# Normed input's two tiles put 96 bytes behind the weights' addresses modulo 128, not 64

## The chip, the cores and the metric

The kernel runs on one core of a Trainium2 chip. The metric is the device time of one execution in microseconds; smaller is better. [...]

## What is computed

Two transformer blocks in float32 on 256 tokens of width 1024, one after the other. The first mixes four branches (a state-space scan and three attentions), the second runs two layers, HGRN2 and then a gated linear recurrence (RG-LRU). Each mixer is followed by a SwiGLU feed-forward of width 2816. Nearly all of the arithmetic is products of a normed input with a large weight matrix:

```python
def rmsnorm(x, w):
    xf = x.astype(jnp.float32)
    y = xf * lax.rsqrt(jnp.mean(xf * xf, axis=-1, keepdims=True) + NORM_EPS)
    return (y * w.astype(jnp.float32)).astype(x.dtype)
...
def swiglu(h, w_gate, w_up, w_down):
    return (jax.nn.silu(h @ w_gate) * (h @ w_up)) @ w_down
...
    h = rmsnorm(x, norm_mix[l])
    x = x + hybrid_mixer(h, w_in[l], ...)
    h = rmsnorm(x, norm_ffn[l])
    x = x + swiglu(h, w_ffn_gate[l], w_ffn_up[l], w_ffn_down[l])
```

## The kernel before

**Weights in units.** Every weight matrix is cut into units (`unit`, `cols`, L210 to L290) of at most 2048 floats in each of 128 partitions, 1 MB. SyncE loads them in order, in two halves, into three rotating slots of the tile `raw` (L2142 to L2160). ScalarE rounds a half to the type fp32r in `whi` (L958), VectorE, or GpSimd in the feed-forwards, puts the rest `raw - whi` in `wlo` (L1359, L1947). The input is split in the same way into a high part and a low part: `hh` and `hl` for the normed input of every mixer and feed-forward (written at L990 and L1383), `bh` and `bl` for the branches' outputs, `eh` and `el` for the inputs of two output products, `ch` and `cl` for a third, `gh` and `gl` for the down products. A product of float32 accuracy is the sum of three fp32r products: high by high, high by low, low by high.

**Two forms of a product.** A matmul loads one operand of 128 x 128 into the array and streams the other past it. In `still` (L480 to L501) the weights are loaded and the input is streamed, 256 columns (the tokens) at a time; its three passes are L492, L495 and L500. A unit of 256 weight columns takes 48 matmuls. `project_columns` and `project_pair` use it on `hh`, `hl` for 112 units and for the half-width unit `dk` (24 matmuls), and `branch` uses it on `bh`, `bl` for 8 units. In `moving` (L503 to L521) the input is loaded and the weights are streamed, 512 columns at a time; its passes are L512, L516 and L520. `project_tokens` uses it on `hh`, `hl` (`z`, `cv`, `bv`, and two each of `hv` and `hg`; two units each, 24 matmuls a unit), and `add_product` on `eh`, `ch` and `gh`. The weights for the next matmul are loaded while the current one streams.

**Order.** Each engine runs its own program; semaphores join them. TensorE goes through the units in order. A feed-forward first has 22 units in the form `still` (the first two as `project_pair`, the other 20 in one stream with the end of that pair: 984 matmuls without other work between), then 11 units in the form `moving`. In the first mixer the streams are short, since attention scores, transposes and value products stand between the units.

**Addresses.** `sbuf` takes tiles from one stack in the order of the calls, each right behind the one before (L84 to L164). All weight slots begin at multiples of 128 bytes in a partition, and all slices that matmuls take of these tiles are multiples of 512 bytes apart, so a tile's address modulo 128 holds for all of its operands. Modulo 128 the tiles begin at: `raw`, `whi`, `wlo`, `x`, `hn`, `eh`, `el` 0; `hh`, `hl` 64 (behind `gap_hh`, 64 bytes); `wrow`, `ident`, `vec`, `st` 64; `diag` and `half` 32; `gate`, `gh`, `gl` 0 (behind `gap_stage`, 288 bytes); `bh`, `bl` 64 (behind `gap_bh`); `ch`, `cl` 0 and `uc` 96; `gw` 0.

Of the kernel before, what the change touches and what calls it, by code (L numbers as in the profile page):

```python
# [72 lines left out]
def build(nc, a):  # L73
    V, A, G, T, S = nc.vector, nc.scalar, nc.gpsimd, nc.tensor, nc.sync
    vq, aq, gq, tq, sq = Waits(V), Waits(A), Waits(G), Waits(T), Waits(S)
    with ExitStack() as root:
# [3 lines left out]
        def sbuf(ctx, name, shape, dt=f32):  # L80
            return ctx.enter_context(nc.sbuf_tensor(name, shape, dt))
# [8 lines left out]
        eh = sbuf(shifted, "eh", [128, 8, 256], f32r)  # L90
        el = sbuf(shifted, "el", [128, 8, 256], f32r)
        shifted.close()
        sbuf(root, "gap_hh", [128, 16])
        hh = sbuf(root, "hh", [128, 8, 256], f32r)
        hl = sbuf(root, "hl", [128, 8, 256], f32r)
        wrow = sbuf(root, "wrow", [128, 2, D])
# [2 lines left out]
        st = sbuf(root, "st", [128, 24])  # L99
        diag = sbuf(root, "diag", [128, 2, 128])  # L100
        half = sbuf(root, "half", [128, 16])
        sbuf(root, "gap_stage", [128, 72])
        banks = [root.enter_context(nc.psum_tensor(f"bank{i}", [128, 512], f32)) for i in range(8)]

        mix = ExitStack()
# [2106 lines left out]
```

## Time and profile before

| | |
|---|---|
| time, median of 3 runs | 1138.95 us (1138.86 to 1139.53) |
| time of the profiled execution | 1138.59 us |
| its span, first to last instruction | 1137.4 us |
| TensorE busy | 1122.9 us, 8117 matmuls |
| VectorE, ScalarE, GpSimd busy | 660.1, 574.5, 297.1 us |
| HBM read | 205.01 MB, 184 GB/s over the span |

Matmuls overlap each other in the array: one is listed from its first to its last part, some 280 ns for 256 columns, though the next begins much sooner. How fast the stream goes is read from the starts in the timeline.

### The profile page before, as it was taken

The page shows a single profiled execution, that of the slowest core. Times are in us where ns is not written, and L with a number is a line of the kernel's source. Part 1 is how long each engine was busy: PE and PEld are TensorE (multiplying, and loading weights), DVE is VectorE, ACT ScalarE, POOL GpSimd, SP SyncE. Part 2 cuts the span into 40 slices and gives each one's busy share as a digit, 9 for nine tenths or more (in the row PEclk, how much of TensorE's full clock was granted, in tenths as well). Part 3 has the DMA queues.
Part 4 walks back from the last instruction along what each step waited for, and adds up shares of the span by engine and source line. Part 5 has one row for each costly group of instructions (what it writes and reads, how often), then busy time and mean ns, then how long its engine had stood idle before and what let it go on. Part 6 is the DMA issues. An engine that isn't in the chain of part 4 may idle for free.

```text
span 1137.4 us, 19300 instructions
## 1 busy us (share of the span) xinstructions
PE 1122.9 (99%) x8117; PEld 1044.9 (92%) x8117; DVE 660.1 (58%) x1039; ACT 574.5 (51%) x878; POOL 297.1 (26%) x193
## 2 busy tenths in 40 slices
PE   8999999999999999999999999999999999999997
PEld 7899989999989999889998889999889979999986
DVE  6755765677675454338897665343238797434324
ACT  6646555555454644436732445444335855544432
POOL 3022100000005444422421114444510003444440
PEclk9999999999999999999999999999999999999999
DMA  8679474554647666655543358665556255765550
GB/s 273 205 250 326 141 241 138 175 153 134 209 151 211 180 188 201 203 185 153 186 165 112 111 164 268 210 189 189 191 180 188 91 182 152 218 189 187 187 183 37
DMA packets 155152, 207.48 MB, mean 182 GB/s; under 512 B 9471, under 2 KB 128409, under 8 KB 155066
## 3 DMA queue, kind: packets, MB, share of 16 engines
q1 hardware_dynamic: 151274, 193.11, 54.2%
q0 software_dynamic: 3792, 13.15, 3.5%
q8 instruction: 64, 1.05, 0.4%
q14 instruction: 22, 0.18, 0.1%
HBM read 205.01 MB, written 4.24 MB: 184 GB/s over the span
## 4 chain that ended last, share of the span: by engine, by line
PE 89%; DVE 7%; ACT 3%; issue 1%; DMA 0%; POOL 0%; SPq 0%; DVEq 0%; ACTq 0%
PE bank L492 18%; PE bank L495 18%; PE bank L500 18%; PE bank L520 9%; PE bank L516 9%; PE bank L512 9%; PE bank L861 3%; DVE wlo L1359 2%; PE bank L787 1%; PE bank L797 1%; ACT whi L958 1%; DVE area L1507 1%; PE bank L562 1%; PE bank L809 1%; DVE uc L1507 0%
## 5 line engine op out<-in xcount | busy, mean ns | idle before, releaser
L1359 DVE TENSOR_TENSOR wlo<-raw,whi 128x1024 fp32r<-128x1024 f32 x275 | 336.2, 1250 | 232.4 <-ACT whi L958 231.6
L958 ACT ACTIVATE whi<-raw 128x1024 fp32r<-128x1024 f32 x362 | 360.5, 1044 | 113.8 <-PE bank L520 107.1
L1947 POOL TENSOR_TENSOR wlo<-raw,whi 128x1024 fp32r<-128x1024 f32 x87 | 223.2, 2565 | 253.8 <-ACT whi L958 253.8
L492 PE MATMUL bank<-hh,whi 128*128 128x256 f32 x1784 | 285.1, 281 | 0.0
L495 PE MATMUL bank<-hh,wlo 128*128 128x256 f32 x1784 | 281.7, 279 | 0.0
L500 PE MATMUL bank<-hl,whi 128*128 128x256 f32 x1784 | 281.5, 279 | 0.0
L492 PEld LDWEIGHTS bank<-hh,whi 128*128 128x128 f32 x1784 | 241.4, 188 | 3.3 <-issue 2.7
L495 PEld LDWEIGHTS bank<-hh,wlo 128*128 128x128 f32 x1784 | 240.8, 188 | 0.0
L500 PEld LDWEIGHTS bank<-hl,whi 128*128 128x128 f32 x1784 | 240.6, 188 | 0.0
L1954 POOL TENSOR_TENSOR st<-st,half 128x1 f32<-128x1 f32 x18 | 10.8, 609 | 334.0 <-DVE st L1376 301.8
L512 PE MATMUL bank<-whi,gh 128*128 128x512 f32 x264 | 81.4, 390 | 0.0
L516 PE MATMUL bank<-wlo,gh 128*128 128x512 f32 x264 | 81.4, 389 | 0.0
L520 PE MATMUL bank<-whi,gl 128*128 128x512 f32 x264 | 81.3, 389 | 0.0
L1188 ACT ACTIVATE sg<-sg 128x512 f32<-128x512 f32 x33 | 20.8, 632 | 95.6 <-DVE sg L1406 95.6
L1192 ACT ACTIVATE gh<-sg 128x512 fp32r<-128x512 f32 x33 | 20.8, 630 | 86.0 <-DVE sg L1740 86.0
L520 PEld LDWEIGHTS bank<-whi,gl 128*128 128x128 f32 x264 | 49.6, 188 | 10.4
L516 PEld LDWEIGHTS bank<-wlo,gh 128*128 128x128 f32 x264 | 49.6, 188 | 10.3
L512 PEld LDWEIGHTS bank<-whi,gh 128*128 128x128 f32 x264 | 49.2, 188 | 9.9
L1740 DVE TENSOR_TENSOR sg<-sg,bank 128x512 f32<-128x512 f32 x33 | 22.7, 688 | 57.4 <-PE bank L500 55.4
L1406 DVE TENSOR_TENSOR sg<-bank,bc_f 128x512 f32<-128x512 f32 x33 | 22.7, 689 | 46.7 <-PE bank L500 46.7
L983 ACT ACTIVATE bank<-x_sb 128x512 f32<-128x512 f32 x26 | 15.6, 600 | 57.6 <-DVE x_sb L1428 29.9
L1742 DVE TENSOR_TENSOR gl<-sg,gh 128x512 fp32r<-128x512 f32 x33 | 30.8, 932 | 23.3 <-ACT gh L1192 23.3
(313 smaller groups left out, 1225.7 us busy)
## 6 DMA issues: line engine op xcount, KB each, us to landing
raw<-in_ffn_w_in SPq DMA_DIRECT2D x88, 512.0 KB, 3.8
raw<-in_w_in SPq DMA_DIRECT2D x72, 512.0 KB, 4.8
raw<-in_ffn_w_out SPq DMA_DIRECT2D x44, 512.0 KB, 3.3
raw<-in_hgrn_w_in SPq DMA_DIRECT2D x32, 512.0 KB, 4.2
raw<-in_w_ffn_gate SPq DMA_DIRECT2D x22, 512.0 KB, 4.7
raw<-in_w_ffn_up SPq DMA_DIRECT2D x22, 512.0 KB, 4.3
raw<-in_w_ffn_down SPq DMA_DIRECT2D x22, 512.0 KB, 3.3
raw<-in_w_branch SPq DMA_DIRECT2D x16, 512.0 KB, 4.4
```

The costliest lines, as they stand in the source:

```text
L492: T.matmul(out, wh[:, i, c], xh[:, k, :], start=first and (i, k) == pairs[0], stop=False)
L495: T.matmul(out, wl[:, i, c], xh[:, k, :], start=False, stop=False)
L500: t = T.matmul(out, wh[:, i, c], xl[:, k, :], start=False, stop=last and (i, k) == pairs[-1])
L512: tok = T.matmul(out, xh[:, k, r], wh[:, i, c], start=first and i == 0, stop=False)
L516: tok = T.matmul(out, xh[:, k, r], wl[:, i, c], start=False, stop=False)
L520: tok = T.matmul(out, xl[:, k, r], wh[:, i, c], start=False, stop=last and i == len(ks) - 1)
L861: tok = T.matmul(banks[b][:, 128 * (2 * h + t):128 * (2 * h + t) + 128], kj[:, h, c], qj[:, h, c], start=True, stop=True)
L958: A.activation(half_of(whi, j, h), half_of(raw, j, h), ACT.Copy).then_inc(s_hi[j % NS][h], 1)
L1359: V.tensor_tensor(half_of(wlo, j, h), half_of(raw, j, h), half_of(whi, j, h).bitcast(f32), ALU.subtract).then_inc(s_lo[j % NS][h], 1)
L1406: V.tensor_tensor(dst, two(bank_of("col", *key)[:, :]), bc[:, :].rearrange("p (o t) -> p o t", o=1).broadcast_to([128, 2, 256]), ALU.mult) ...
L1742: V.tensor_tensor(gl[:, 2 * j:2 * j + 2, :], two(s), gh[:, 2 * j:2 * j + 2, :].bitcast(f32), ALU.subtract).then_inc(s_gl, 1)
L1947: G.tensor_tensor(half_of(wlo, j, 1), half_of(raw, j, 1), half_of(whi, j, 1).bitcast(f32), ALU.subtract).then_inc(s_lo[j % NS][1], 1)
```

## The change

The unused tile `gap_hh` in front of `hh` has 24 floats in place of 16, and `gap_stage` 64 in place of 72. `hh`, `hl`, `wrow`, `ident`, `vec`, `st`, `diag` and `half` begin 32 bytes later; `gate` and all that follows stay where they were. Instructions, waits and transfers are the same.

```diff
@@ -90,7 +90,7 @@
         eh = sbuf(shifted, "eh", [128, 8, 256], f32r)
         el = sbuf(shifted, "el", [128, 8, 256], f32r)
         shifted.close()
-        sbuf(root, "gap_hh", [128, 16])
+        sbuf(root, "gap_hh", [128, 24])
         hh = sbuf(root, "hh", [128, 8, 256], f32r)
         hl = sbuf(root, "hl", [128, 8, 256], f32r)
         wrow = sbuf(root, "wrow", [128, 2, D])
@@ -99,7 +99,7 @@
         st = sbuf(root, "st", [128, 24])
         diag = sbuf(root, "diag", [128, 2, 128])
         half = sbuf(root, "half", [128, 16])
-        sbuf(root, "gap_stage", [128, 72])
+        sbuf(root, "gap_stage", [128, 64])
```

## Rows read from the trace of the kernel before

**Rows 1.** The page: head, TensorE's busy us and share, granted clock by slice.

```profile
span 1137.4 us, 19300 instructions
...
PE 1122.9 (99%) x8117; PEld 1044.9 (92%) x8117; DVE 660.1 (58%) x1039; ACT 574.5 (51%) x878; POOL 297.1 (26%) x193
...
PEclk9999999999999999999999999999999999999999
```

**Rows 2.** The page: the chain that ended last, by engine and by line.

```profile
PE 89%; DVE 7%; ACT 3%; issue 1%; DMA 0%; POOL 0%; SPq 0%; DVEq 0%; ACTq 0%
PE bank L492 18%; PE bank L495 18%; PE bank L500 18%; PE bank L520 9%; PE bank L516 9%; PE bank L512 9%; PE bank L861 3%; DVE wlo L1359 2%; PE bank L787 1%; PE bank L797 1%; ACT whi L958 1%; DVE area L1507 1%; PE bank L562 1%; PE bank L809 1%; DVE uc L1507 0%
```

**Rows 3.** Waits of PE, longest first: us in total, times, longest us.

```profile
PE bank L632 <- DMA wrow<-in_norm_mix: 2.2, 1, 2.2
PE bank L640 <- DVE hn L1470: 1.8, 1, 1.8
```

**Rows 4.** Timeline (start us, length us, matmuls merged): `still`, first feed-forward.

```profile
344.71 0.63 PE L492 MATMUL bank<-hh,whi 128*128 128x256 f32 x4
...
458.72 0.63 PE L500 MATMUL bank<-hl,whi 128*128 128x256 f32 x4
```

**Rows 5.** Timeline: `still` on the same tiles, in the first mixer.

```profile
174.31 0.62 PE L495 MATMUL bank<-hh,wlo 128*128 128x256 f32 x4
...
177.48 0.62 PE L500 MATMUL bank<-hl,whi 128*128 128x256 f32 x4
```

**Rows 6.** Timeline: `still` on `bh` and `bl`, two streams.

```profile
188.11 0.40 PE L492 MATMUL bank<-bh,whi 128*128 128x256 f32 x2
...
189.52 0.40 PE L492 MATMUL bank<-bh,whi 128*128 128x256 f32 x2
...
195.40 0.39 PE L492 MATMUL bank<-bh,whi 128*128 128x256 f32 x2
...
196.76 0.28 PE L492 MATMUL bank<-bh,whi 128*128 128x256 f32 x1
```

**Rows 7.** Timeline: `moving` with `hh` loaded, product `z`.

```profile
41.95 1.09 PE L516 MATMUL bank<-wlo,hh 128*128 128x512 f32 x4
...
45.68 1.09 PE L520 MATMUL bank<-whi,hl 128*128 128x512 f32 x4
```

**Rows 8.** Timeline: `moving` with `gh` loaded, first down product.

```profile
461.94 0.62 PE L512 MATMUL bank<-whi,gh 128*128 128x512 f32 x2
...
464.66 0.62 PE L512 MATMUL bank<-whi,gh 128*128 128x512 f32 x2
```

**Rows 9.** Timeline: `moving` with `eh` loaded, behind a group of transposes.

```profile
657.42 0.63 PE L516 MATMUL bank<-wlo,eh 128*128 128x512 f32 x2
...
660.20 0.62 PE L516 MATMUL bank<-wlo,eh 128*128 128x512 f32 x2
...
661.12 0.61 PE L512 MATMUL bank<-whi,eh 128*128 128x512 f32 x2
...
662.48 0.61 PE L512 MATMUL bank<-whi,eh 128*128 128x512 f32 x2
```

**Rows 10.** By line: duration ns (min/median/max), first and last start us.

```profile
L492 PEld LDWEIGHTS bank<-hh,whi x1784: 186/188/192, 17.5 to 1070.1; 128*128 128x128 f32 x199
L492 PE MATMUL bank<-hh,whi x1784: 276/279/467, 17.6 to 1070.2; 128*128 128x256 f32 x199
...
L512 PEld LDWEIGHTS bank<-whi,gh x264: 187/188/192, 459.1 to 1129.8; 128*128 128x128 f32 x132
L512 PE MATMUL bank<-whi,gh x264: 389/389/476, 459.2 to 1130.0; 128*128 128x512 f32 x132
...
L512 PE MATMUL bank<-whi,hh x128: 228/394/483, 35.6 to 641.8; 128*128 128x512 f32 x112, 128*128 128x144 f32 x16
...
L929 PE MATMUL bank<-uc,gw x64: 377/379/379, 883.3 to 896.9; 128*128 128x256 f32 x64
```

**Rows 11.** Stretches: length us, each engine's busy us, clock, DMA share, GB/s.

```profile
343.40:459.10 115.70, 115.70 (x985) 115.70 (x984) 57.05 (x78) 60.25 (x71) 54.99 (x22) 1.00 0.65 193
460.50:514.90 54.40, 54.40 (x242) 45.04 (x241) 19.07 (x19) 20.96 (x27) 18.33 (x7) 1.00 0.57 184
```

## The prediction

> **What bounds the kernel now.** The page's head and busy lines come first [rows 1]: a span of 1137.4 us, in which TensorE streams matmuls for 1122.9 us (99%). [...] The chain that ended last says the same thing by line: 89% of it is PE, and L492, L495 and L500, the three passes of `still`, hold 18% each [rows 2]. The waits of TensorE are small: the longest two are 2.2 and 1.8 us [rows 3]. So the time is the number of matmuls times the beat, by which I mean the distance from one matmul's start to the next, and the beat is what I read next, in the timeline. "Mean ns of one" in the grouped view won't do for it: it is a latency, and neighbours overlap.
>
> **The beats.** In the stretch of 984 `still` matmuls of the first feed-forward, 968 of them lie between the starts 344.71 and 458.72: 114.01 / 968 = 117.8 ns [rows 4]. [...] But from 174.31 to 177.48, 28 matmuls of the same form on the same tiles take 3.17 us, 113.2 ns each [rows 5]. There are thus two steady beats, and a stream keeps the one that it starts with. The fast one holds in eight streams only: the one at 119.23 (96 matmuls), those at 173.74, 180.87, 208.39, 233.09, 246.84 and 274.37 (48 each) and the one at 524.01 (54): 438, of which the first of a stream has another gap, so about 424 steady gaps. The matmuls on `bh`, which has the same 64 bytes modulo 128, do both as well: 12 from 188.11 take 1.41 us (117.5 ns), 12 from 195.40 take 1.36 us (113.3 ns) [rows 6]. [...] With `hh` loaded its beat is 3.73 us / 16 = 233.1 ns [rows 7]; with `gh`, at offset 0 modulo 128, it is 2.72 / 12 = 226.7 ns [rows 8]. With `eh`, also at offset 0, 12 matmuls from 657.42 take 2.78 us (231.7 ns), and a few matmuls later 6 take 1.36 us (226.7 ns): there the slow beat dissolves by itself [rows 9]. The durations by line agree: a 512-column matmul is listed at 389 ns at the median with `gh` and 394 ns with `hh`, while the weight load has its median at 188 ns whether `gh` is loaded or the weights for `still` are [rows 10].
> Two things follow. [...] And what lies above it is a loss per weight load: 117.8 - 113.3 = 4.5 ns in `still` (4.44 by the unrounded starts of the long stretch), 233.1 - 226.7 = 6.4 ns in `moving` with `hh`. The streamed operand and the load for the next matmul read SBUF at the same time, and the loss depends on how the two are set against each other, in time (two beats at one offset) and, by rows 7 to 9, in address.
>
> **The change, part by part.** (1) `gap_hh` grows by 32 bytes and `gap_stage` shrinks by 32. `hh` and `hl` move from 64 to 96 behind the weight tiles modulo 128, and everything from `gate` on stays. No instruction, wait or DMA is added or removed, so whatever changes must come from address effects. (2) `still` on `hh`/`hl`: 112 column units of 48 matmuls and the half-width `dk` of 24, 5,400 matmuls, less the 424 at the floor: about 4,960 at the slow beat (some 16 gaps are stream starts). If offset 96 frees them: 4,960 x 4.44 = 22.0 us. (3) `moving` with `hh` loaded: 7 products of 2 parts x 2 x 12 = 336 matmuls; at best 336 x 6.4 = 2.2 us. (4) `wrow`, `ident`, `vec`, `st`, `diag` and `half` move along by 32 bytes. `ident` is streamed by 200 transposes; at the loss just found, about 5 ns each, they are worth at most 1 us either way. The VectorE and ScalarE work that reads or writes these tiles lies beside matmuls: in the stretch 343.40 to 459.10 ACT is busy for 60.25 of 115.70 us and DVE for 57.05, while PE is full [rows 11]. I cost it at nothing; that cover would have to shrink by half before it is felt. (5) What is late next, if the beat falls by 4%: DMA. It is busy 65% of that stretch at 193 GB/s [rows 11]; 4% more is 201 GB/s, and in the `gh` stretch the same unit of weights already goes by at the fast beat without a wait of TensorE [rows 3, 11]. So the gain is passed on in full.
> No fp32r row of the trace has an offset of 96, so its beat is unknown, and I bound it from both sides. Below: the floor, 113.3 ns. Above: the loss per load could be that of `hh` in `moving`, 6.4 ns, giving 119.7 ns; or twice today's, 8.9 ns. [...] With the two beats at 64 showing that a small shift is enough to leave the loss, I take the floor.
> The kernel then stands at 1138.6 (the profiled execution's own time; its span is 1137.4) - 22.0 - 2.2 = 1114.4 us. The profiled execution is 0.4 us under the median of 1138.95, so on the median's scale that is 1114.8. Some starts of streams will pay a few slow beats before they settle, as `eh` does, where 12 beats cost 12 x 5.0 ns = 0.06 us [rows 9]: for some 40 streams that is 2.4 us at most, and I take half, 1.2 us. Forecast: 1116 us.
> [...]
>
> **The rivals.**
> A (forecast), offset 96 frees most streams: 1116 us, 1111 to 1120 with the spread of the starts. [...]
> B, a lottery at each start: the beat is chosen by how a stream starts, and 96 only changes the odds, so that about half of the matmuls go free: 1138.95 - 12 = 1127 us (1120 to 1136). For it: `bh` in both beats at one offset [rows 6].
> C, nothing: offset has no part in it, only the timing at a stream's start, and 32 bytes more change none of that; or addresses count only in steps of 64 bytes. Then 1139 us (1136.7 to 1141.2). For it: rows 6 again, and weight loads of equal length in both forms. Against it: `gh` and `eh` settle at the floor and `hh` in `moving` never does. [...]
> D, the other side, slower: at 96 the streamed reads meet the weight reads more often, everywhere. The price by the `moving` row is 6.4 ns per load instead of 4.44: 4,960 x 1.96 = 9.7 us, and the 424 that are free today lose 6.4 ns, 2.7 us: 1138.95 + 12.4 = 1151 us. With twice today's loss it is 22.0 + 3.8 = 25.8 and 1165 us. It decides from the point at which the beat passes 117.8 ns. For it: 64 is half of the period, which keeps the two readers as far apart in address as they can be, and 96 brings them nearer. Against: today's distance doesn't save 92% of the matmuls from the loss.
>
> **How the numbers follow.** A 0.42, B 0.10, C 0.17, D 0.31. Faster by over 0.2% (2.3 us, about what a measurement of this kernel can tell from no change) is A and B: 0.52; within it C: 0.17; slower D: 0.31. The range runs from A's lower end, 1111, to D's lower price with room, 1158; outside it lies most of D at twice the loss. The likeliest case's own range is 1111 to 1120.
>
> **What would show it.** Right: in the timeline, 28 `still` matmuls on `hh` take 3.17 us nearly everywhere, above all in the three streams of 984; L492's matmuls are listed at 276 ns at the median, not 279; 512-column matmuls with `hh` at 389, not 394; `bh`, `gh` and `eh` as before. B would show streams of both beats, C the same starts as now, D 119 ns and more. If PE waits for DMA or for the low parts appear in the place of the gain, step (5) is wrong. The forecast is wrong at its root if 96 has a loss of its own, which no row here can exclude.

## The result, and the profile after

The changed kernel takes 1152.35 us at the median (before: 1138.90), a ratio of 1.0116 with a 95% interval of 1.0102 to 1.0129: it is slower by 1.2%. That median counts one disturbed execution, the profiled one (2253.6 us; the beat of its long streams was 233.5 to 233.6 ns); the other three took 1151.38, 1151.43 and 1153.27 us, and the profile shown here is that of a repeat of the same kernel, which took 1151.45 us at the median (ratio 1.0112, 1.0097 to 1.0127).

The page of the repeat: head, busy time, granted clock and the chain by line, answering to [rows 1, 2].

```profile
span 1150.6 us, 19300 instructions
...
PE 1137.8 (99%) x8117; PEld 1060.0 (92%) x8117; DVE 660.4 (57%) x1039; ACT 574.7 (50%) x878; POOL 298.5 (26%) x193
...
PEclk9999999999999999999999999999999999999999
...
PE bank L492 19%; PE bank L500 19%; PE bank L495 19%; PE bank L516 9%; PE bank L520 9%; PE bank L512 9%; PE bank L861 2%; PE bank L929 1%; DVE wlo L1359 1%; PE bank L787 1%; PE bank L797 1%; PE bank L562 1%; PE bank L809 1%; DMA x_sb<-in_x 0%; PE bank L884 0%
```

The span is 13.2 us longer and TensorE is busy 14.9 us more, with the same 8117 matmuls; DVE and ACT moved by 0.3 us or less. The shares of L492, L495 and L500 grow. The time is all in the beat. The timeline of the stream of 984 in the first feed-forward and of a stream in the first mixer, answering to [rows 4, 5]:

```profile
349.19 0.64 PE L495 MATMUL bank<-hh,wlo 128*128 128x256 f32 x4
...
466.79 0.63 PE L512 MATMUL bank<-whi,gh 128*128 128x512 f32 x2
```
```profile
178.34 0.64 PE L495 MATMUL bank<-hh,wlo 128*128 128x256 f32 x4
...
181.70 0.64 PE L500 MATMUL bank<-hl,whi 128*128 128x256 f32 x4
```

The first row is the fifth matmul of the stream and the second is the first one behind it: 980 gaps in 117.60 us are 120.0 ns, where [rows 4] had 117.8. In the mixer 28 gaps take 3.36 us, 120.0 ns too, where [rows 5] had 113.2. No stream on `hh` has the fast beat any more. By line, answering to [rows 10]:

```profile
L492 PE MATMUL bank<-hh,whi x1784: 277/282/468, 18.2 to 1083.5; 128*128 128x256 f32 x199
...
L512 PE MATMUL bank<-whi,gh x264: 389/389/476, 466.8 to 1143.3; 128*128 128x512 f32 x132
L512 PE MATMUL bank<-whi,hh x128: 227/397/479, 36.6 to 650.2; 128*128 128x512 f32 x112, 128*128 128x144 f32 x16
```

The median of L492 went from 279 to 282 ns and that of the form `moving` with `hh` from 394 to 397; `gh`, which did not move, stays at 389. The sum: 4,960 x 2.2 ns = 11.0 us for the matmuls that were at 117.8, 424 x 6.7 = 2.8 us for those that lose the fast beat, 336 x 0.8 = 0.3 us in `moving` (mean gap 234.3 against 233.5 ns): 14.1 us. Against it stands some 0.8 us by which TensorE, being later, waits less for wlo (1.6 to 1.4 us) and cl (1.0 to 0.4); the span grew by 13.2.

### The profile page after: what moved, and what is told of

Same layout as the page of the kernel before. It is cut to its first block, busy times and chain, and to the rows that moved or that the text cites. A ratio compares the mean times of both kernels' runs of the same rounds, so it can differ in the third digit from the quotient of the medians.

```text
span 2252.3 us, 19300 instructions
## 1 busy us (share of the span) xinstructions
PE 2241.7 (100%) x8117; PEld 1953.9 (87%) x8117; DVE 652.1 (29%) x1039; ACT 580.4 (26%) x878; POOL 285.1 (13%) x193
## 4 chain that ended last, share of the span: by engine, by line
PE 99%; DMA 0%; DVE 0%; ACT 0%; issue 0%; SPq 0%; POOL 0%; DVEq 0%
PE bank L492 20%; PE bank L500 20%; PE bank L495 20%; PE bank L516 10%; PE bank L512 10%; PE bank L520 10%; PE bank L861 3%; PE bank L929 1%; PE bank L562 1%; PE bank L787 1%; PE bank L797 1%; PE bank L809 1%; PE bank L884 0%; PE bank L812 0%; PE bank L570 0%; DMA x_sb<-in_x 0%
## 5 line engine op out<-in xcount | busy, mean ns | idle before, releaser
L492 PE MATMUL bank<-hh,whi 128*128 128x256 f32 x1784 | 514.0, 444 | 0.0
L495 PE MATMUL bank<-hh,wlo 128*128 128x256 f32 x1784 | 509.0, 438 | 0.0
L500 PE MATMUL bank<-hl,whi 128*128 128x256 f32 x1784 | 508.1, 440 | 0.0
L492 PEld LDWEIGHTS bank<-hh,whi 128*128 128x128 f32 x1784 | 466.4, 348 | 10.0 <-issue 9.2
L500 PEld LDWEIGHTS bank<-hl,whi 128*128 128x128 f32 x1784 | 469.4, 350 | 0.0
L495 PEld LDWEIGHTS bank<-hh,wlo 128*128 128x128 f32 x1784 | 468.7, 349 | 0.0
L516 PE MATMUL bank<-wlo,gh 128*128 128x512 f32 x264 | 150.8, 677 | 0.0
L520 PE MATMUL bank<-whi,gl 128*128 128x512 f32 x264 | 150.8, 674 | 0.0
L512 PE MATMUL bank<-whi,gh 128*128 128x512 f32 x264 | 150.7, 673 | 0.0
L512 PE MATMUL bank<-whi,hh 128*128 128x512 f32 (+1 forms) x128 | 63.6, 650 | 0.0
```

Source lines behind the costliest of these rows:

```text
L492: T.matmul(out, wh[:, i, c], xh[:, k, :], start=first and (i, k) == pairs[0], stop=False)
L495: T.matmul(out, wl[:, i, c], xh[:, k, :], start=False, stop=False)
L500: t = T.matmul(out, wh[:, i, c], xl[:, k, :], start=False, stop=last and (i, k) == pairs[-1])
L512: tok = T.matmul(out, xh[:, k, r], wh[:, i, c], start=first and i == 0, stop=False)
L516: tok = T.matmul(out, xh[:, k, r], wl[:, i, c], start=False, stop=False)
L520: tok = T.matmul(out, xl[:, k, r], wh[:, i, c], start=False, stop=last and i == len(ks) - 1)
```

## The experiments

All versions differ from the kernel before in unused tiles alone, if nothing else is said. A gap of unused floats behind `hl` puts `wrow` and the tiles behind it back where they were modulo 128. Modulo 256 they lie 128 bytes further in some versions (96 with the tiles put back, 16, 48, 128, 160, 192 and `hl` alone); a run below that moves only them shows no effect of it. "Beat" is the mean gap of `still` in the streams of 984, from their starts in the timeline.

**Where in the change the loss is.** First the changed kernel again, then with the tiles that moved along put back:

```diff
-        sbuf(root, "gap_hh", [128, 16])
+        sbuf(root, "gap_hh", [128, 24])
...
+        sbuf(root, "gap_wrow", [128, 24])
         wrow = sbuf(root, "wrow", [128, 2, D])
...
-        sbuf(root, "gap_stage", [128, 72])
+        sbuf(root, "gap_stage", [128, 40])
```

> The changed kernel once more, for a profile at full TensorE clock. In all theories about 1151 to 1153 us. If the loss per weight load grew (rival D), the beat of the long streams of still on hh lies at 119.5 to 121 ns, where it was 117.8, and bh, gh and eh keep 113.3 / 117.8 and 226.7. If a part of the streams only left the fast beat and paid for more starts, the long streams stay at 117.8 ns.

> hh and hl at 96 as in the change, but wrow, ident, vec, st, diag and half back at their old offsets modulo 128 (another unused tile of 96 bytes stands behind hl). Theory 'matmul on hh': as the changed kernel, 1150 to 1154 us. Theory 'the tiles that moved along': back to about 1139 us.

Measured: 1151.45 and 1151.65 us, 120.0 ns in both. The moved `ident`, `wrow` and `st` cost nothing that can be measured; the loss is in the matmuls on `hh` and `hl`.

**Other offsets.** The same edit with other gaps (`gap_hh` none at 0, 8 floats at 32, up to 72 floats at 288). For the offsets 16, 48 and 80 the gaps stay multiples of 32 bytes; each tile has 8 floats of room instead and is used from its fifth float on:

```diff
-        hh = sbuf(root, "hh", [128, 8, 256], f32r)
-        hl = sbuf(root, "hl", [128, 8, 256], f32r)
+        hh_room = sbuf(root, "hh", [128, 2056], f32r)
+        sbuf(root, "gap_hl", [128, 24])
+        hl_room = sbuf(root, "hl", [128, 2056], f32r)
+        hh = hh_room[:, 4:2052].rearrange("p (k t) -> p k t", t=256)
+        hl = hl_room[:, 4:2052].rearrange("p (k t) -> p k t", t=256)
```

> hh and hl at offset 0 modulo 128 from the weights, all other tiles at their old offsets. Theory 'nearness' (the loss grows as the streamed reads and the weight reads come nearer modulo 128; 64 is farthest): slower than at 96, above 1153 us, perhaps 1165; moving with hh loaded goes down to 226.7 ns all the same. Theory 'block edge' (only the place within 64 bytes counts): about 1139 us or a little less, since moving gains 2 us.

> hh and hl at offset 32, all other tiles at their old offsets. Theory 'nearness': the same distance as 96 on the other side, so 1150 to 1154 us. Theory 'block edge': the same place within 64 bytes as 96, so 1150 to 1154 us too. A theory in which the direction matters (the streamed reads ahead of the weight reads or behind them) gives another time than at 96, by more than 5 us.

> hh and hl at 48 behind the weights modulo 128 (each lies 16 bytes into a tile with room), all else as before. Known by now: beats of still of 120.0 ns at 0, 116.7 at 32, 117.8 (or 113.3) at 64, 120.0 at 96. Theory 'smooth' (the loss follows the offset continuously, lowest between 32 and 64): a beat of 116 ns or less, under 1136 us, and this offset beats both. Theory 'steps of 32' (an address counts by its block of 32 bytes): 116.7 ns, about 1136 us. Theory 'off the 32-byte edge costs': above 117.8 ns, over 1139 us.

> hh and hl at 80. 'Smooth': between the 117.8 ns of 64 and the 120.0 of 96, so about 118.9 ns and 1145 us. 'Steps of 32': as 64, 117.8 ns and 1139 us. 'Off the edge costs': 120 ns or more, over 1150 us.

> hh and hl at 16. 'Smooth': between the 120.0 ns of 0 and the 116.7 of 32, so about 118.3 ns and 1142 us. 'Steps of 32': as 0, 120.0 ns and 1149 us.

> hh and hl at 160, that is 32 modulo 128. If the period is 128 bytes the beat is 116.7 ns and the time that of offset 32, 1136 us. If it is longer (256 or more), any of the other beats may come: over 2 us from 1136.

> hh and hl at 192, which is 64 modulo 128. Offset 160 did not repeat 32 (118.7 ns against 116.7), so the period is longer than 128. If it is 256 or more, 192 needn't repeat the 117.8 / 113.3 ns of 64; by the fall from 96 (120.0) over 160 (118.7) I expect 116 to 119 ns, 1132 to 1145 us. If 160 differed for another reason and 128 is the period after all: 117.8 ns, 1139 us.

> hh and hl at 288, that is 32 modulo 256. If the period is 256 bytes the beat is 116.7 ns and the time 1136 us as at 32; if it is longer, another beat, over 2 us away.

> hh and hl at 128. Between 96 (120.0 ns) and 160 (118.7) if the map is smooth: about 119.5 to 120 ns, 1147 to 1150 us. With a period of 128 bytes it would repeat offset 0 exactly: 120.0 ns for every gap, 1149.3 us.

> hh and hl at 224, between 192 (the floor, 113.3 ns) and 256, which is 0 (120.0 ns). Smooth: about 116.7 ns, 1136 us. If the loss-free place is wider than one step: 113.3 ns, about 1123 us. If 224 repeated 96, as a period of 128 would have it: 120.0 ns, 1151 us.

Measured, in the order of the offset; the last column is the mean gap of `moving` with `hh` loaded (512 columns). In the rows 16, 48 and 80 the room and `gap_hl` put `hl` 8320 bytes behind `hh`, which is 65 x 128: modulo 256 `hl` lies there at 144, 176 and 208, so these three rows mix two offsets:

| `hh`, `hl` at | time us | ratio (95%) | beat ns | `moving` ns |
|---|---|---|---|---|
| 0 | 1149.26 | 1.0092 (1.0077 to 1.0107) | 120.0 | 227.4 |
| 16 (`hl` 144) | 1139.70 | 1.0007 (0.9997 to 1.0017) | 117.5 | 233.2 |
| 32 | 1136.13 | 0.9976 (0.9967 to 0.9986) | 116.7 | 233.2 |
| 48 (`hl` 176) | 1140.59 | 1.0014 (1.0005 to 1.0024) | 117.8 | 232.0 |
| 64 (before) | 1138.90 | 1 | 117.8 (or 113.3) | 233.5 |
| 80 (`hl` 208) | 1142.96 | 1.0035 (1.0022 to 1.0048) | 118.3 | 232.1 |
| 96 (the change) | 1151.45 | 1.0112 (1.0097 to 1.0127) | 120.0 | 234.3 |
| 128 | 1145.97 | 1.0061 (1.0046 to 1.0076) | 118.7 | 232.4 |
| 160 | 1144.20 | 1.0045 (1.0030 to 1.0060) | 118.7 | 233.3 |
| 192 | 1123.36 | 0.9866 (0.9849 to 0.9882) | 113.3 | 229.2 |
| 224 | 1142.89 | 1.0034 (1.0022 to 1.0047) | 118.3 | 233.3 |
| 288 | 1136.03 | 0.9978 (0.9969 to 0.9988) | 116.7 | 233.3 |

Timelines of the first stream of 984: offset 0 (from its thirteenth matmul, 972 gaps), 32, 192 and 224 (from the fifth, 980 gaps), each to the first matmul behind it.

```profile
348.80 0.64 PE L493 MATMUL bank<-hh,whi 128*128 128x256 f32 x4
...
465.44 0.63 PE L513 MATMUL bank<-whi,gh 128*128 128x512 f32 x2
```
```profile
345.45 0.63 PE L496 MATMUL bank<-hh,wlo 128*128 128x256 f32 x4
...
459.78 0.40 PE L513 MATMUL bank<-whi,gh 128*128 128x512 f32 x1
```
```profile
343.24 0.62 PE L495 MATMUL bank<-hh,wlo 128*128 128x256 f32 x4
...
454.31 0.63 PE L512 MATMUL bank<-whi,gh 128*128 128x512 f32 x2
```
```profile
346.50 0.63 PE L496 MATMUL bank<-hh,wlo 128*128 128x256 f32 x4
...
462.46 0.63 PE L513 MATMUL bank<-whi,gh 128*128 128x512 f32 x2
```

116.64 / 972 = 120.0, 114.33 / 980 = 116.7, 111.07 / 980 = 113.3 and 115.96 / 980 = 118.3 ns. What falls: that the loss depends on the distance between the two readers alone (0 and 96 are equal, 32 and 96 are not, nor 32 and 224); that only the place in a block of 64 bytes counts (0 against 64); and that the period is 128 bytes. By that, 128 should repeat 0, 160 repeat 32 and 224 repeat 96, and they give 118.7 for 120.0, 118.7 for 116.7 and 118.3 for 120.0. 288 repeats 32 in beat and time, so 256 bytes is a period that all these rows agree with. The steps of 16 show less, since `hl` moved by 128 bytes more than `hh`. But the gaps of the `hh` matmuls alone, taken from their starts, average 117.8 ns at 16, against 120.0 at 0, so the address does not count by its block of 32 either.

**What makes the loss.** At offset 0 the gaps of the long streams are 120 ns (2,930 of the 2,937 behind the fourth matmul of each), so this is where half of a weight load can be taken away. The third pass loads 64 columns instead of 128, except for the last matmul of a group (L502 in this kernel; L504 is the last one):

```diff
+                        if xl is hl and (i, k) != pairs[-1]:
+                            t = T.matmul(out[0:64, :], wh[:, i, 128 * m:128 * m + 64], xl[:, k, :], start=False, stop=last and (i, k) == pairs[-1])
+                        else:
+                            t = T.matmul(out, wh[:, i, c], xl[:, k, :], start=False, stop=last and (i, k) == pairs[-1])
```

> Offset 0, where every gap of still on hh is 120.0 ns (6.7 over the floor). In the third pass on hl all matmuls but the last of each group load only 64 of the 128 weight columns: hl by the upper 64 columns' weights is left out of the product, so the output is less accurate; this is not the reference's output. The stream of 256 columns is unchanged. Theory 'the loss is made by the reads of the weight load beside the stream': the gap of the matmul during which a half load runs falls by half of the loss, to about 116.7 ns, for some 1,550 matmuls: 1149.3 - 5.2 = 1144 us. Theory 'the loss belongs to the stream's own address': all gaps stay at 120.0 and the time at 1149 us.

```profile
399.13 0.63 PE L496 MATMUL bank<-hh,wlo 128*128 128x256 f32 x4
399.61 0.63 PE L502 MATMUL bank<-hl,whi 128*64 128x256 f32 x4
400.07 0.64 PE L493 MATMUL bank<-hh,whi 128*128 128x256 f32 x4
400.55 0.64 PE L496 MATMUL bank<-hh,wlo 128*128 128x256 f32 x4
401.03 0.51 PE L502 MATMUL bank<-hl,whi 128*64 128x256 f32 x3
```

Measured: 1139.82 us, 9.4 less than with whole loads. In these rows the pass of 4 gaps that begins with the half loads takes 0.46 us (from 399.61 to 400.07, 115 ns a gap), the others 0.48 us (120 ns). By the starts in the three long streams, the gap before a matmul with a half load averages 116.8 ns: half of the 6.7 ns is gone, as expected. What was not expected is that the other gaps fell too, to 118.6 ns on average, although their own loads are whole; the mean of the streams is 118.05 ns. That is why the kernel gained 9.4 us and not 5.2; how a half load reaches the gaps beside it isn't shown. The input streamed is the same in both versions, so the loss does not belong to the stream alone. One thing isn't separated here: a matmul with 64 loaded columns also writes 64 rows of its bank instead of 128. That the loads' reads make the loss, and not the writes, rests on the runs in which an address moves and nothing else (117.8 ns before, 116.7 with the loaded tiles alone moved, below).

**One pair or the whole stream.** `hl` alone at 96 (a gap of 8 floats between `hh` and `hl`):

> hh stays at 64, hl alone goes to 96. Theory 'each gap's loss is that of its own pair of operands': two thirds of the gaps as at 64 (117.8), one third as at 96 (120.0): a mean of 118.5 ns, 1143 us. Theory 'the stream locks as a whole': one of the two beats, 117.8 or 120, for all three passes, or a new one.

```profile
400.26 0.63 PE L497 MATMUL bank<-hh,wlo 128*128 128x256 f32 x4
400.73 0.64 PE L502 MATMUL bank<-hl,whi 128*128 128x256 f32 x4
401.21 0.63 PE L494 MATMUL bank<-hh,whi 128*128 128x256 f32 x4
401.68 0.63 PE L497 MATMUL bank<-hh,wlo 128*128 128x256 f32 x4
```

1142.51 us, 12 gaps in 1.42 us, 118.3 ns: near the mixture of 118.5. By the starts in the three long streams, the gaps of matmuls that stream `hl` average 120.0 ns, which is the beat of 96, and those that stream `hh` 117.5, close to the 117.8 of 64. So each gap's loss is that of its own operands, within 0.3 ns. It is the mean that follows them: single gaps of these streams run from 114 to 125 ns.

**The difference of the addresses, or the address.** The weights move by 32 bytes, the input stays:

```diff
+        sbuf(root, "gap_whi", [128, 8])
         whi = sbuf(root, "whi", [128, NS, UC], f32r)
...
+        sbuf(root, "gap_x", [128, 56])
         x = sbuf(root, "x_sb", [128, 2, D])
```

> whi and wlo lie 32 bytes further, hh, hl, bh and bl where they were (64 in the old count), so still has a difference of 32. Theory 'difference': its long streams go at 116.7 ns, as with the input at 32. Theory 'address of the streamed tile': 117.8 ns as before. The form moving with gh or eh loaded has its streamed tile moved from 0 to 32: up to 6.5 ns more for 792 + 288 matmuls, so the whole kernel may end up slower than the beat of still alone would give: 1135 to 1142 us.

The stream of 984 from its thirteenth matmul (972 gaps), and `gh` in `moving`:

```profile
346.00 0.63 PE L494 MATMUL bank<-hh,whi 128*128 128x256 f32 x4
...
459.39 0.63 PE L514 MATMUL bank<-whi,gh 128*128 128x512 f32 x2
...
470.58 0.63 PE L514 MATMUL bank<-whi,gh 128*128 128x512 f32 x2
...
471.99 0.63 PE L514 MATMUL bank<-whi,gh 128*128 128x512 f32 x2
```

113.39 / 972 = 116.7 ns, the beat of offset 32; the streams on `bh`, whose tile did not move either, go at 116.7 as well. The difference counts. With `gh` loaded and the moved weights streamed, 6 gaps now take 1.41 us; over all its streams the mean is 233.3 ns, where [rows 8] has 226.7. That costs the 1,080 matmuls of `gh`, `eh` and `ch` about 6.5 ns each and makes the whole slower: 1141.59 us (ratio 1.0025, 1.0015 to 1.0034).

**Why 192 is fast.** It has the same two beats as 64: its long streams go at 113.3, but 20 shorter ones on `hh` (of 48 matmuls and more) at 117.8. And that version had moved `ident`, `wrow` and `st` from 64 to 192 modulo 256. Each alone:

> hh and hl stay at 64; wrow, ident, vec, st, diag and half alone go 128 bytes further, to 192 modulo 256. Theory 'the start decides' (64 and 192 are one offset with two beats, 117.8 and 113.3, and what TensorE did just before picks one): the three streams of 984 go at 113.3 ns, 1122 to 1126 us. Theory 'offset 192 of hh': nothing moves, 1139 us.

> hh and hl at 192, but wrow, ident, vec, st, diag and half at 64 modulo 256 as in the kernel before. Theory 'offset 192 of hh', with a period of 256: as the version at 192, 113.3 ns in the long streams and 1123 us. Theory 'the start decides', with a period of 128: as the kernel before, 117.8 ns and 1139 us.

The first gives 1139.39 us (ratio 1.0006, 0.9997 to 1.0016) and 117.8 ns in all three long streams. The second gives 1126.77 us (0.9892, 0.9876 to 0.9909); its timeline at the first and the second of the long streams:

```profile
341.93 0.64 PE L496 MATMUL bank<-hh,wlo 128*128 128x256 f32 x4
...
457.36 0.63 PE L513 MATMUL bank<-whi,gh 128*128 128x512 f32 x2
...
680.17 0.62 PE L496 MATMUL bank<-hh,wlo 128*128 128x256 f32 x4
...
791.24 0.63 PE L513 MATMUL bank<-whi,gh 128*128 128x512 f32 x2
```

115.43 / 980 = 117.8 ns in the first, 111.07 / 980 = 113.3 in the second (and in the third). Neither theory holds alone. The place of `hh` decides most of it: at 64 it is 0 of 3 long streams with the rest in either place, at 192 it is 2 or 3 of 3. Of the 5,400 matmuls on `hh`, some 440 lie in fast streams before, some 3,300 with 192 alone and some 4,200 with the rest moved too. What settles the others isn't shown; the place of the rest is one thing that changes it. At 192 many streams begin with one to three gaps of 116 to 123 ns and then go over to 113; at 64 the 982 gaps never do.

**`bh` and `bl` too.** They go to 192 as well (`gap_bh` 48 floats for 16):

> hh, hl and also bh, bl at 192 behind the weights modulo 256. If the map of offsets is one of the form still and not of the tile, the streams on bh that ran at 117.8 ns (in the version with hh alone at 192 all six did) fall to 113.3: at most 384 x 4.4 = 1.7 us, so 1121.7 to 1123.4 us. If a short stream behind attention work stays at the beat with which it starts, nothing is gained: 1123.4.

1122.76 us, a ratio of 0.9858 (0.9844 to 0.9873): 16.2 us less than before. The 0.6 us under the version with `hh` at 192 is not clear of the noise, since the two intervals overlap. Two of the seven streams on `bh` have the fast beat, where the version with `hh` at 192 has none; but with `bh` at 64 the kernel before has three. That 192 is better than 64 is shown for `hh`, and not for `bh`.

## Why the prediction was wrong

It forecast 1116 us and gave the slower side 0.31; the kernel took 1152.35 us.

What bounds the kernel: right. The beat of `still` and `moving` on `hh` is the time. Whatever moved it moved the span, from 113.3 to 120.0 ns, and no engine behind took back a gain: at 192 the longest waits of TensorE are 2.5 and 2.3 us, so step (5) held, though in versions other than this one.

The floor: held. It was the fastest beat of the rows, 113.3 ns, half the 226.7 of `gh`, and no offset tried has a steady beat under it. That it is the least which fp32r can do isn't shown.

The step that failed is the one that put offset 96 at the floor. With it the forecast took 22.0 us off for the matmuls of `still`. No run shows this term; the runs show 13.8 us more for them in its place (11.0 and 2.8). It rested on the author's thought that a small shift would be enough to leave the loss; no fp32r row of before has 96, so none shows it. Measured, the loss at 96 rises by half, 4.4 to 6.7 ns. The bounds around it were sound: the nearer upper one, 6.4 ns or 119.7 ns, is within 0.3 ns of the 120.0 measured, and rival D's price at it, 1151 us, is within 1.4 us of the result. The chances failed, not the prices. D's argument (64 is as far apart as can be) was wrong all the same: 192 is as far modulo 256 and reaches the floor in its long streams, and 0 and 96 are equally bad.

That D's price came out so near is in part luck: it was borrowed from `moving`, whose own loss at 96 is 7.6 ns and not 6.4, and `moving` and `still` have different maps of offsets.

Step (3), `moving` with `hh`: expected -2.2 us, measured +0.3. Step (4), the other tiles: right, nothing that can be measured. The allowance for starts had nothing to apply to, since no stream on `hh` settled at the floor. Rival C is refuted: the offset does count. So do the loads of the next weights in these fp32r matmuls: moving the tile that they read, while the streamed tile stayed, took the beat from 117.8 to 116.7 ns, and halving the loads gave back 9.4 us. Rival B, the lottery at the start, fits 64 and 192, where streams on one offset have 117.8 or 113.3 ns, and had no part at 96, where each long stream has 120.0.

One premise was taken from the change's own words and never questioned: that addresses count modulo 128. The trace of before could not show it, for the split tiles of its products differ from the weights by 0 or 64, and `uc` from `gw` by 96, modulo 128 and modulo 256 alike.

## What to carry to other kernels

Where TensorE is full and the operands are fp32r, read the beat from the starts in the timeline and compare it with the fastest beat that the same form has anywhere in the trace, here 113.3 ns for 256 columns and 226.7 for 512; what was above it depended on the difference between the address of the streamed tile and that of the tile being loaded. Try differences over 256 bytes rather than guess: here 32 bytes more cost 1.2% and 128 bytes more gained 1.3%, with no instruction changed. Check that both tiles of a split input have the same difference: with `hl` alone at 96 the gaps on it took 120.0 ns, those on `hh` 117.5. And a steady beat seen in a few streams, as 113.3 ns in eight on `hh` before, is worth a search for what makes it common.

## What was not expected of the hardware

The beats of `still` lie at 113.3, 116.7, 117.5, 117.8, 118.3, 118.7 and 120.0 ns, and a kernel repeats its own within 0.02 ns in all three long streams, except the one with 192 alone, which has both 117.8 and 113.3. One offset can hold two of them, settled in the first few gaps and kept for 980 matmuls. `moving` with the same tile has another map: it is close to its floor (227.4 against 226.7) at 0, where `still` is at its worst, so of the offsets tried none is best for both forms; 192 is the best for `still` and second best for `moving` (229.2). What makes the beats repeat after 256 bytes (116.7 ns at 32 and at 288), and what in a stream's start picks the beat, stays open.
